# Decay rows brought head by head, the distance table spread inside DRAM during fox heads, Toeplitz tiles loaded one by one: a two-block transformer kernel on one core

## The reference

```python
def fox_mixer(h, ...):                  # first block: 16 heads of 128
    q, k, v, f_logit = split(h @ w_in)
    q, k = rms_norm(q), rms_norm(k)
    cum = cumsum(log_sigmoid(f_logit + b_f))            # one decay row of 256 per head
    s = q @ k.T * scale + (cum[..., :, None] - cum[:, :, None, :])
    return softmax(where(causal, s, -inf)) @ v @ w_out

def gla_mixer(q, k, v, r, log_g): ...   # second block, 4 heads, chunked gated linear attention
def dilated_mixer(q, k, v, rel_bias):   # second block, 8 heads: a bias per head
    ...                                 # that depends on the distance query - key alone
def conv_ffn(h): ...                    # first block:  silu(gate) * val after a width-3 convolution
                                        # second block: silu(gate) * up
```

## Time and profile before

| | |
|---|---|
| median of 3 runs | 2342.95 us (2339.54 to 2345.64) |
| the profiled execution: its time, its span | 2339.76 us, 2338.0 us |
| mean granted PE clock | 0.997 |
| busy share PE, PE weight load, DVE, ACT, POOL | 99%, 85%, 69%, 52%, 0% |
| read from DRAM, written to it | 418.98 MB, 3.69 MB |

### The profile page before, as it was taken

How to read it: one execution, slowest core, us unless ns; L and a number is a source line. 1 busy time by engine, 2 the same in 40 slices (tenths; PEclk the granted TensorE clock), 3 DMA queues, 4 the chain that set the end, 5 groups by cost and what they waited for, 6 DMA issues and landing times.

```text
span 2338.0 us, 39013 instructions
## 1 busy us (share of the span) xinstructions
PE 2309.1 (99%) x13218; PEld 1996.5 (85%) x13218; DVE 1609.9 (69%) x2339; ACT 1219.7 (52%) x1574; POOL 10.4 (0%) x22
## 2 busy tenths in 40 slices
PE   7899999999999999999999999999999999999999
PEld 6788888888888888888887888888888888888888
DVE  6577777788888888555566667677666666665554
ACT  6566665555555555444455466655444444443332
POOL 0000000000000000000000000000000000000000
PEclk9999999999999999999999999999999999999999
DMA  6644445555555555555554544455555555555554
GB/s 229 172 156 160 161 156 175 181 191 187 188 192 191 184 190 194 188 188 187 189 187 144 170 153 161 161 181 188 190 188 189 188 189 189 189 189 198 197 197 135
DMA packets 118048, 423.37 MB, mean 181 GB/s; under 512 B 13597, under 2 KB 15789, under 8 KB 117872
## 3 DMA queue, kind: packets, MB, share of 16 engines
q1 hardware_dynamic: 114048, 415.29, 54.3%
q0 software_dynamic: 1504, 5.12, 1.0%
q10 hardware_dynamic: 2448, 2.32, 0.3%
HBM read 418.98 MB, written 3.69 MB: 181 GB/s over the span
## 4 chain that ended last, share of the span: by engine, by line
PE 95%; DMA 2%; DVE 2%; ACT 1%; issue 1%; SPq 0%; DVEq 0%; ACTq 0%
PE acc L331 61%; PE acc L332 30%; DMA raw<-wstream 2%; PE b_mean L357 1%; DVE wlo L923 1%; PE b_score L368 0%; DMA xres<-xt 0%; PE b_turn L376 0%; ACT whi L640 0%; PE b_mean L449 0%; PE b_mean L450 0%; PE b_score L367 0%; PE b_mean L382 0%; PE b_mean L383 0%; PE b_mean L384 0%
## 5 line engine op out<-in xcount | busy, mean ns | idle before, releaser
L331 PE MATMUL acc<-xs,whi 128*128 128x512 f32 x4384 | 1552.7, 399 | 14.9 <-DVE wlo L923 12.4
L640 ACT ACTIVATE whi<-raw 128x1024 fp32r<-128x1024 f32 x788 | 831.0, 1059 | 881.1 <-PE acc L332 847.9
L923 DVE TENSOR_TENSOR wlo<-raw,whi 128x1024 fp32r<-128x1024 f32 x788 | 961.0, 1222 | 417.4 <-ACT whi L640 414.5
L332 PE MATMUL acc<-xs,wlo 128*128 128x256 f32 x4384 | 1221.2, 279 | 0.0
L331 PEld LDWEIGHTS acc<-xs,whi 128*128 128x128 f32 x4384 | 825.4, 188 | 217.6 <-DVE wlo L923 14.4
L332 PEld LDWEIGHTS acc<-xs,wlo 128*128 128x128 f32 x4384 | 827.4, 189 | 5.8 <-issue 5.6
L331 PE MATMUL acc<-hid,whi 128*128 128x512 f32 x1408 | 491.3, 393 | 0.0
L332 PE MATMUL acc<-hid,wlo 128*128 128x256 f32 x1408 | 394.5, 280 | 0.0
L929 DVE TENSOR_REDUCE folded_t<-acc 128x256 f32<-128x512 f32 (+1 forms) x338 | 233.0, 689 | 159.3 <-PE acc L332 143.7
L331 PEld LDWEIGHTS acc<-hid,whi 128*128 128x128 f32 x1408 | 264.9, 188 | 61.0
L332 PEld LDWEIGHTS acc<-hid,wlo 128*128 128x128 f32 x1408 | 263.6, 187 | 0.0
(11 more groups left out here) (168 smaller groups left out, 915.3 us busy)
## 6 DMA issues: line engine op xcount, KB each, us to landing
raw<-wstream SPq DMA_DIRECT2D x788, 512.0 KB, 4.2
xres<-xt SPq DMA_DIRECT2D x4, 512.0 KB, 8.1
decay_row<-decay_scratch POOLq DMA_DIRECT2D x1, 2048.0 KB, 11.7
out<-xres ACTq DMA_DIRECT2D x16, 128.0 KB, 3.0
dist_scratch<-dist_bias POOLq DMA_DIRECT2D x1, 1536.0 KB, 41.0
toeplitz<-dist_scratch POOLq DMA_DIRECT2D x8, 128.0 KB, 4.0
vec<-vectors ACTq DMA_DIRECT2D x1, 213.5 KB, 5.1
g_keep<-scan_keep POOLq DMA_DIRECT2D x1, 128.0 KB, 3.2
```

Of the source, the lines that this page charges most:

```text
L331: pe.matmul(acc[bank_no][:, :], w_hi, x[:, kc, :, :].rearrange("p a s -> p (a s)"), start=first, stop=False)
L332: mm = pe.matmul(acc[bank_no][:, S:2 * S], w_lo, x[:, kc, 0, :], start=False, stop=last)
L640: act.activation(whi[slot][:, :], raw[slot][:, :], ACT.Copy).then_inc(hi_ready, 1)
L923: dve.tensor_tensor(wlo[slot][:, :], raw[slot][:, :], whi[slot][:, :], ALU.subtract).then_inc(lo_ready, 1)
```

## The change

The 2 MB read of `decay_row` becomes 16 reads of 128 KB. Each is issued when the one before it has landed, and from head 2 on also not before PE has finished head h - 2. DVE no longer waits for all rows before the fold at step 2 of head 1; `softmax_max` waits for the row of its own head in each head. `dist_bias` is written to DRAM once (`bias_scratch`, 12 KB), behind the third decay row, and spread to 128 rows by one DRAM-to-DRAM transfer of 192 KB for each dilated head, behind the decay rows of heads 8 to 15. The Toeplitz reads wait for PE's progress: one for every four units from the second GLA head on, each also behind the landing of the one before.

```diff
+        bias_dram = nc.dram_tensor("bias_scratch", [DIL_HEADS, TOEPLITZ], F32)
...
-            bring(decay_row[:, :, :], bass.AP(decay_dram, 0, [[0, P], [S, FOX_HEADS], [1, S]]), decay_landed)
-
-            pool.wait_ge(bias_out, 1)
-            bring(dist_dram[:, :, :], dist_bias[:, :].rearrange("h (a w) -> h a w", a=1).to_broadcast([DIL_HEADS, P, TOEPLITZ]),
-                  bias_stored)
-
-            pool.wait_ge(bias_stored, 16)
+            for h in range(FOX_HEADS):
+                if h:
+                    pool.wait_ge(decay_landed, 16 * h)
+                if h >= 2:
+                    pool.wait_ge(unit_used, L0.unit_heads + HEAD_UNITS * (h - 1))
+                bring(decay_row[:, h, :], bass.AP(decay_dram, h * S, [[0, P], [1, S]]), decay_landed)
+                if h == 2:
+                    pool.wait_ge(bias_out, 1)
+                    bring(bias_dram[:, :], dist_bias[:, :], bias_stored)
+                    pool.wait_ge(bias_stored, 16)
+                g = h - DIL_HEADS
+                if g >= 0:
+                    if g:
+                        pool.wait_ge(dist_spread, 16 * g)
+                    bring(dist_dram[g, :, :], bass.AP(bias_dram, g * TOEPLITZ, [[0, P], [1, TOEPLITZ]]), dist_spread)
+
+            pool.wait_ge(dist_spread, 16 * DIL_HEADS)
             pool.wait_ge(unit_used, L1.unit_in)
...
             for h in range(DIL_HEADS):
-
+                pool.wait_ge(unit_used, L1.unit_heads + GLA_UNITS + 4 * h)
+                if h:
+                    pool.wait_ge(toeplitz_landed, 16 * h)
                 bring(toeplitz[:, h, :], bass.AP(dist_dram, (h * P * TOEPLITZ) + P - 1, [[TOEPLITZ - 1, P], [1, S]]), toeplitz_landed)
...
                     if run.kind == "fox":
+                        if t == 0:
+                            dve.wait_ge(decay_landed, 16 * (h + 1))
                         table = decay_row[:, h, 0:b - a]
...
-                if (j, s) == (1, 2):
-                    dve.wait_ge(decay_landed, 16)
```

More of the change, by code:

```diff
@@ L235, in build @@
         out_stored = sem("out_stored")
+        dist_spread = sem("dist_spread")
         def column(name, c=0):
```

## The result

| | before | changed |
|---|---|---|
| median of 5 runs | 2342.95 us (2339.54 to 2345.64) | 2330.62 us (2330.52 to 2330.68) |
| ratio | | 0.995 (95% interval 0.9939 to 0.996) |
| the profiled execution's span | 2338.0 us | 2328.8 us |

The account below looks back on a forecast made before the run. PE bounds the kernel, busy 99%, with gaps where weights wait beside the two table transfers. Recovering 12.50 us less 0.1 for contention gives -12.4 us, median 2342.95 to 2330.5 us, range 2325.5 to 2337.

Parts of the forecast that it names:

- the 12.4: Whole kernel: predicted gain of 12.4 us, from 12.50 us recovered less 0.1 us for contention of small transfers.
- What was lost in heads 1 and 2: Heads 1 and 2 took 51.44 us and should take 38.94, so 12.50 us were lost.
- the one term: Heads 1 and 2: PE's idle time and the lower-clock matmuls behind it counted together as 12.50 us.
- the narrow place: Distance table's source, 8 SBUF partitions on two ports: 53 GB/s, about 29.9 us, weights at half of what they need.
- would stand behind it: Weight transfers at 62 to 84 us: the weights' rows on the table's partitions would queue behind the table; weights got 85 GB/s.
- Decay rows: Sixteen 128 KB reads from 43.3 us on: 4.0 us each, cost on PE's path 0.
- Spreads: Heads 8 to 15, 192 KB each inside DRAM: 3 to 5 us each, cost to PE 0.
- Toeplitz reads: Start of second block: gaps there belong to the gate sums, so cost 0 and gain 0.
- DVE's instruction: One register instruction and one wait in each of 14 loop heads: at most 3.9 us on DVE, 0 on the path.
- the 12 KB store: Store of the biases to DRAM from the same 8 partitions, 1/128 of what moved before: cost 0.
- The rules against the change: Batching rule: 23 additional transfers, 46 us, 2389 us if on the path; shared-port rule: DVE delays POOL's small reads. Predicted cost 0.
- slow-spread rival: Heads 8 to 15: slow DRAM spreads stall PE beyond 7.4 us spare; at 20 us each, 2348 us; chance 0.03.

Follow-up runs that it names:

- the pair of sources: Changed kernel, but the 1.5 MB table spread in one transfer behind decay row 2: from SBUF 2343.43 us, from the 12 KB DRAM copy 2331.20 us.
- the pair of partition sets: Table spread from SBUF behind decay row 2 (2343.43 us from partitions 0 to 7), source moved to 32 partitions: 2335.27 us; to 8 partitions four apart: 2329.21 us.
- the single read: Changed kernel, but all 16 decay rows in one 2 MB read with one DVE wait: 2327.68 us, and 2330.68 us when run again.
- the burst run: Changed kernel, but the eight Toeplitz reads issued back to back at the start of the second block, as before: 2331.13 us.
- the early run from SBUF: Changed kernel, but the 1.5 MB distance table spread straight from 8 SBUF partitions in one transfer behind decay row 2: 2343.43 us.
- the late run: Changed kernel, but the 1.5 MB table spread from SBUF in one transfer behind decay row 8 instead of 2: 2346.13 us.

## Why the prediction was right, point by point

- **The time.** Forecast 2330.5 us, measured 2330.62. That the medians agree to 0.1 us is luck by the steps: against its own execution of 2339.76 us, which had none, I forecast 2327.4 us, and the profiled execution of the changed kernel, with one step, has a span 9.2 us shorter, not 12.4. Without that step the mark says 12.3 us, and this is what bears out the 12.4.
- **What was lost in heads 1 and 2.** Forecast 12.50 us less 0.1; the two heads shortened by 51.44 - 39.09 = 12.35 us. The three heads from 44.09 us took 19.31, 19.78 and 19.75 us, forecast 19.1, 19.8 and 19.8. Counting the slow matmuls behind the gap into the one term was right: the clock is 1.00 throughout now.
- **The cause.** The prediction named the table's 8 partitions as the narrow place, from 53 GB/s with the DMA engines 63% busy. This is shown by the pair of sources, by the pair of partition sets, and by the kernel before with the source alone changed. One step of it the traces don't bear out: the weights' rows on those partitions "would stand behind it". Rows 8 give 0.234 x 16 x 22 / 509 = 0.16 us for a weight packet beside the table and 0.495 x 16 x 60 / 2703 = 0.18 us without it, so no weight packet was slow; a table packet took 0.381 x 16 x 22 / 225 = 0.60 us of an engine.
- **Decay rows.** Forecast 4.0 us each and no cost on the path; measured 3.5 us (3.2 to 5.1), no DVE wait for them. Their split was costed at nothing, which held; the single read shows also that it earned nothing. The prediction had left open which of the two transfers made the loss; the whole of it was the table.
- **Spreads.** Forecast 3 to 5 us each; 3.7 measured, and the weights landed in 3.1 to 4.7 us from 190 to 340 us.
- **Toeplitz reads, DVE's instruction, the 12 KB store.** Forecast 0; the burst run and the windows show 0.
- **The rules against the change.** The Trainium skill, "DMA: Bandwidth & Descriptors", section "Bandwidth", asks to batch transfers to at least 1 MiB. The price of not doing so was real in latency and free in time: sixteen reads of 3.5 us are 56 us in place of 11.7, all beside PE's work. The Trainium skill, "SBUF — State Buffer", section "SBUF: two separate sides", says that DVE can hold up transfers that GpSimd issues, while it has the port that the two share. No sign of it appeared: the sixteen reads landed in 3.2 to 5.1 us, with DVE busy 214.69 of 304.00 us from 96 to 400. Whether any instruction of DVE takes that port here is not shown.
- **Where a size was wrong.** The working of the slow-spread rival says that "a transfer of T us at the old sharing delays the weights by 0.48 T", with 7.4 us spare. It has two faults. It counts PE's idle time alone. In the early run from SBUF, T = 35.0 us gives 9.4 us, and I had expected 5 to 8; PE stood 4.34 + 3.47 = 7.8 us from 60 to 110 us, but 12.7 us were lost. The other 4.9 us go with matmuls at a lower clock behind the gaps (0.96 and 0.84 granted in the two windows), a cost that the 12.50 us of the forecast had in it and this working left out. And its sharing is not a constant. In the late run, T = 33.8 us gives 8.8 us, PE stood 11.4 us, and 15.4 were lost. There the weights got 1.27 MB in 25 us, 51 GB/s, not the 85 of before. With 51 the working gives (1 - 51 / 164) x 33.8 - 7.4 = 15.9 us; that this is near the 15.4 is luck, since it stands for the 11.4 us of idle time. Why the weights kept 85 GB/s in the one place and 51 in the other is not settled. No forecast for this change hung on it, since no such transfer is left in it.

## What to carry to other kernels

When a transfer slows its neighbours, look at the DMA share beside the GB/s. Here engines busy 0.64 of the time moved 125 GB/s from the narrow source and, busy 0.66, 231 GB/s from DRAM: the same share with half the rate meant packets that each took long. The first thing to look at is then how many partitions the source has and how far apart they stand. Repeat small rows from a DRAM copy, or from partitions four apart, rather than from neighbours. When a loss is forecast, count the slower matmuls behind a gap with the gap: they were 4.0 and 4.9 us beside 11.4 and 7.8 idle. And when a change has several parts, run the smallest alone: here the table's source was the whole gain.

## What the runs showed of the hardware that I had not expected

- Eight neighbouring partitions gave 45 GB/s (1.57 MB in 35.0 us), eight partitions four apart 88 GB/s, 32 partitions 118 GB/s (13.3 us, in another shape), one partition alone 22 GB/s (197 KB in 8.8 us), all from issue to landing and beside the weight stream.
- Weight packets took 0.16 to 0.20 us with and without the slow table beside them, while whole weight loads took up to 28.0 us instead of 3.3: what a narrow source costs its neighbours is turns, not packet time.
- The down stages run at one of two rates from their first to their last unit: 288 or 289 matmuls in 50 us, or 285, with PE full and the clock at 1.00 in both. A stage has 88 units of 16 matmuls, 1,408; at 50 / 288 and 50 / 285 us each that is 244.4 or 247.0 us, 2.6 us apart by counts that are rounded to one matmul, where mark and spans show 3.1. Two such stages make times that come in steps: 2327.2, 2330.7 and 2333.9 us for the one with a single decay read. The 6 us between the fastest and the slowest of the five runs of before would be two steps, but its runs don't fall into steps as clearly (2341.91 and, in a later batch, 2337.53 to 2343.42 us), so the loss itself seems to have varied.
